# Retention in three fp32r passes: where the kernel now splits scores, masked scores and values into high and low parts

## The reference

```
scores = einsum('bhid,bhjd->bhij', qc, kc) * intra
out    = einsum('bhij,bhjv->bhiv', scores, vc) + einsum('bhid,bhdv->bhiv', qc * q_decay, state)
ret    = head_layer_norm(retention(rq, rk, rv)) * silu(rg)
```

## Time and profile before

| | before |
|---|---|
| median of 3 runs | 2162.86 us (2162.66 to 2163.64) |
| the profiled execution | 2162.67 us |
| its span in the profile | 2160.9 us |
| TensorE matmuls busy | 2127.8 us, 98% |
| VectorE busy | 1155.5 us, 53% |
| ScalarE busy | 775.7 us, 36% |
| granted TensorE clock, mean | 0.998 |

### The profile page before, as it was taken

The page is one execution under the profiler, slowest core; times in us unless marked ns, Lnnn a source line. Parts: engine busy times, 40 slices in busy tenths (PEclk is TensorE's granted clock), DMA queues, the critical chain, the costliest instruction groups (busy, mean ns, idle before and its releaser), DMA issues.

```text
span 2160.9 us, 33274 instructions
## 1 busy us (share of the span) xinstructions
PE 2127.8 (98%) x13064; PEld 1840.4 (85%) x13064; DVE 1155.5 (53%) x1731; ACT 775.7 (36%) x1218; POOL 51.3 (2%) x79
## 2 busy tenths in 40 slices
PE   9999999999999999999999999999999989999998
PEld 8988888788888788888888888989999988889896
DVE  6553334534556455544535666357855557446364
ACT  4222222422444444322324566344433343222233
POOL 0000000000000000000000000012300000000000
PEclk9999999999999999999999999999999999999999
DMA  4222221222222322222223221231133212232222
GB/s 148 97 98 96 93 74 68 89 97 79 75 71 68 107 93 94 98 94 99 88 97 97 79 90 59 83 115 60 55 144 98 88 68 82 95 97 89 96 89 96
DMA packets 52969, 194.71 MB, mean 90 GB/s; under 512 B 6896, under 2 KB 7280, under 8 KB 52224
## 3 DMA queue, kind: packets, MB, share of 16 engines
q1 hardware_dynamic: 49248, 177.56, 24.7%
q10 hardware_dynamic: 2656, 12.41, 1.5%
q0 software_dynamic: 960, 3.24, 0.5%
HBM read 186.77 MB, written 6.42 MB: 89 GB/s over the span
## 4 chain that ended last, share of the span: by engine, by line
PE 94%; DVE 3%; ACT 2%; issue 0%; DMA 0%; SPq 0%; DVEq 0%; ACTq 0%
PE ps L1811 77%; PE ps L2341 5%; PE ps L2208 1%; PE ps L1998 1%; PE ps L2023 1%; PE ps L1961 1%; PE ps L2273 1%; PE ps L2114 1%; DVE kk_r L1456 1%; PE ps L2037 1%; ACT kk L726 1%; ACT kk L727 0%; PE ps L2251 0%; PE ps L2095 0%; PE ps L1940 0%
## 5 line engine op out<-in xcount | busy, mean ns | idle before, releaser
L429 ACT ACTIVATE wh<-wraw 128x1024 fp32r<-128x1024 f32 x330 | 348.4, 1056 | 903.1 <-PE ps L1811 794.8
L986 DVE TENSOR_TENSOR wl<-wraw,wh 128x1024 fp32r<-128x1024 f32 x330 | 403.2, 1223 | 140.9 <-ACT wh L429 133.5
L1811 PE MATMUL ps<-xh,wh 128*128 128x264 f32 (+1 forms) x2056 | 392.4, 336 | 5.9 <-ACT wh L429 2.0
L1811 PE MATMUL ps<-xh,wl 128*128 128x264 f32 (+1 forms) x2056 | 385.6, 332 | 0.0
L1811 PE MATMUL ps<-xl,wh 128*128 128x264 f32 (+1 forms) x2056 | 385.4, 332 | 0.0
L1811 PEld LDWEIGHTS ps<-xh,wh 128*128 128x128 f32 x2056 | 312.5, 188 | 49.4 <-issue 4.8
L1811 PEld LDWEIGHTS ps<-xh,wl 128*128 128x128 f32 x2056 | 314.4, 188 | 39.6
L1811 PEld LDWEIGHTS ps<-xl,wh 128*128 128x128 f32 x2056 | 314.3, 188 | 39.7
L1811 PE MATMUL ps<-bh,wh 128*128 128x264 f32 (+1 forms) x1296 | 234.2, 325 | 2.8 <-DVE hf L1019 1.7
L1811 PE MATMUL ps<-bl,wh 128*128 128x264 f32 (+1 forms) x1296 | 231.0, 322 | 0.0
L1811 PE MATMUL ps<-bh,wl 128*128 128x264 f32 (+1 forms) x1296 | 230.6, 322 | 0.0
(11 more groups left out here) (424 smaller groups left out, 2010.4 us busy)
## 6 DMA issues: line engine op xcount, KB each, us to landing
wraw<-weights_dram SPq DMA_DIRECT2D x331, 512.0 KB, 3.5
hf<-tables_dram POOLq DMA_DIRECT2D x12, 264.0 KB, 3.1
res<-x_t_dram SPq DMA_DIRECT2D x4, 528.0 KB, 7.1
res<-x_t_dram ACTq DMA_DIRECT2D x1, 2112.0 KB, 9.0
res_dram<-res ACTq DMA_DIRECT2D x1, 2112.0 KB, 6.5
mrg_dram<-mrg ACTq DMA_DIRECT2D x1, 2112.0 KB, 7.3
mrg<-mrg_dram ACTq DMA_DIRECT2D x1, 2112.0 KB, 8.8
res<-res_dram ACTq DMA_DIRECT2D x1, 2112.0 KB, 16.0
```

The lines of the kernel that those rows point to most:

```text
L429: nc.scalar.activation(wh[:, slot], wraw[:, slot], ACT.Copy).then_inc(hi_done, 1)
L986: nc.vector.tensor_tensor(wl[:, slot], wraw[:, slot], wh[:, slot].bitcast(F32), ALU.subtract)\
L1811: last = nc.tensor.matmul(o, w[:, slot, c, :], a[:, c, tok], start=(k == 0), stop=(k == len(steps) - 1))
```

## The change

Scores and products of retention are done in three fp32r passes. ScalarE makes the high parts of q and k (turns with step 2 and 3 of the head before, for q and k apart), of the five pieces of the masked scores and of the centred values (both in step 1); VectorE makes the low parts, in the place of the values themselves. The high parts of q, k and the scores lie in `bh`, those of the values in `bl`, which are free until the gated rows are written there. TensorE issues three matmuls where one plain fp32 matmul stood. `products(h, v)` now waits for the low parts of the scores (`ra_lo`) and for the high parts of its values (`rv_hi`), and before its third pass for their low parts (`rv_lo`).

```diff
+        def attention_part(t):
+            q0 = first_query(t)
+            if t == 4:
+                return atm[0:NM, 0:NM], atm_hi[:, :], atm_lo[:, :]
+            return at[:, t, q0:SEQ], at_hi[:, t, q0:SEQ], at_lo[:, t, q0:SEQ]
+        def value_parts(h, v):
+            f, g = slice(RDV * h + P * v, RDV * h + P * v + P), slice(P * v, P * v + P)
+            x, r, y = vt[:, :, f], vtr[:, :, f], values_hi[h % 2][:, :, g]
+            return (x[:, 0:4], y[:, 0:4], r[:, 0:4]), (x[0:NM, 4], y[0:NM, 4], r[0:NM, 4])
...
 ScalarE, turn i, after split_hi
+                h, step = divmod(i - 2, 4)
+                if step < 2 and 0 <= h < RH:
+                    n = RSTRIP + 4 * h + step
+                    act.wait_ge(evicted[n % 2], n // 2 + 1)
+                    if step == 0:
+                        nc.scalar.activation(q_hi[:, NM:T], qq[:, h, NM:T], ACT.Copy).then_inc(rqk_hi, 1)
+                    else:
+                        nc.scalar.activation(k_hi, qq[:, 4 + h, :], ACT.Copy).then_inc(rqk_hi, 1)
                 h, step = divmod(i - 4, 4)
                 if step == 1 and 0 <= h < RH:
+                    for t in range(5):
+                        whole, high, _ = attention_part(t)
+                        act.wait_ge(rs_masked, 5 * h + t + 1)
+                        nc.scalar.activation(high, whole, ACT.Copy).then_inc(ra_hi, 1)
                     for v in range(2):
...
+                    act.wait_ge(centred, h + 1)
+                    for v in range(2):
+                        for whole, high, _ in value_parts(h, v):
+                            ins = nc.scalar.activation(high, whole, ACT.Copy)
+                        ins.then_inc(rv_hi, 1)
...
 VectorE, step 1
+                    attention_low(h)
                     centred_values(h)
+                    values_low(h, 0)
+                    values_low(h, 1)
...
             def products(h, v):
-                pe.wait_ge(centred, h + 1)
+                pe.wait_ge(ra_lo, 5 * h + 5)
+                pe.wait_ge(rv_hi, 2 * h + v + 1)
...
+                for k in range(3):
+                    if k == 2:
+                        pe.wait_ge(rv_lo, 2 * h + v + 1)
+                    V, A = (1, 1, 2)[k], (1, 2, 1)[k]
+                    for t in range(4):
+                        q0 = first_query(t)
+                        nc.tensor.matmul(ps[:, 5 + v, q0:SEQ], main[V][:, t], attention_part(t)[A], start=(t == k == 0),
+                                         stop=False)
```

More of the change, by code:

```diff
@@ L137, in build @@
         wh, wl = sb("wh", [P, 2, KC, P], F32R), sb("wl", [P, 2, KC, P], F32R)
-        qq = sb("qq", [P, KC, T])
+        qq, qqr = shared("qq", [P, KC, T])
         kk, kkr = shared("kk", [P, KC, T])
-        vt = sb("vt", [P, 5, D])
+        vt, vtr = shared("vt", [P, 5, D])
         mrg = sb("mrg", [P, KC, T])
-        res = sb("res", [P, KC, T])
+        res, resr = shared("res", [P, KC, T])
         tmp = sb("tmp", [P, 2, T])
@@ L237, in build @@
         rz_ready, rs_masked, ro_ready, ro_copied = (sem(n) for n in ("rz_ready", "rs_masked", "ro_ready", "ro_copied"))
+        rqk_hi, rqk_lo, ra_hi, ra_lo, rv_hi, rv_lo = (sem(n) for n in ("rqk_hi", "rqk_lo", "ra_hi", "ra_lo", "rv_hi",
+                                                                      "rv_lo"))
         centred, rsq_added, rsum_done, r_scaled = (sem(n) for n in ("centred", "rsq_added", "rsum_done", "r_scaled"))
@@ L306, in scores_ap @@
             return (ps[:, 2, :], ps[:, 3, 0:400], ps[:, 4, 0:272], ps[:, 4, 272:416], ps[0:NM, 4, 416:432])[t]
+        at_lo, atm_lo = flat(resr)[:, 0:4 * SEQ].rearrange("p (k q) -> p k q", k=4), flat(resr)[0:NM, 4 * SEQ:4 * SEQ + NM]
+        at_hi, atm_hi = flat(bh)[:, 0:4 * SEQ].rearrange("p (k q) -> p k q", k=4), flat(bh)[0:NM, 4 * SEQ:4 * SEQ + NM]
+        q_hi, k_hi = flat(bh)[:, 4 * T:5 * T], flat(bh)[:, 5 * T:6 * T]
+        values_hi = [flat(bl)[:, 5 * RDV * k:5 * RDV * (k + 1)].rearrange("p (t f) -> p t f", t=5) for k in range(2)]
+        def attention_part(t):
[7 more added lines that the diff above has]
+            return (x[:, 0:4], y[:, 0:4], r[:, 0:4]), (x[0:NM, 4], y[0:NM, 4], r[0:NM, 4])
         ret_silu = {21: (0, 1, 2), 22: (3, 4, 5), 23: (6,), 24: (7,)}
@@ L1200, in centred_values, with attention_low, values_low @@
                     .then_inc(centred, 1)
+            def attention_low(h):
+                for t in range(5):
+                    whole, high, low = attention_part(t)
+                    dve.wait_ge(ra_hi, 5 * h + t + 1)
+                    nc.vector.tensor_tensor(low, whole, high.bitcast(F32), ALU.subtract).then_inc(ra_lo, 1)
+            def values_low(h, v):
+                dve.wait_ge(rv_hi, 2 * h + v + 1)
+                for whole, high, low in value_parts(h, v):
+                    ins = nc.vector.tensor_tensor(low, whole, high.bitcast(F32), ALU.subtract)
+                ins.then_inc(rv_lo, 1)
             for i in range(N_RET + 3):
@@ L1207, in _ @@
                     split_lo(n, n // 2, n % 2)
+                h, step = divmod(i - 2, 4)
+                if step < 2 and 0 <= h < RH:
+                    dve.wait_ge(rqk_hi, 2 * h + step + 1)
+                    if step == 0:
+                        nc.vector.tensor_tensor(qqr[:, h, NM:T], qq[:, h, NM:T], q_hi[:, NM:T].bitcast(F32), ALU.subtract)\
+                            .then_inc(rqk_lo, 1)
+                    else:
+                        nc.vector.tensor_tensor(qqr[:, 4 + h, :], qq[:, 4 + h, :], k_hi.bitcast(F32), ALU.subtract)\
+                            .then_inc(rqk_lo, 1)
                 h, step = divmod(i - 4, 4)
@@ L1931, in scores @@
             def scores(h):
-                for j in (4 * h, 4 * h + 1, 4 * h + 2):
-                    n = RSTRIP + j
-                    pe.wait_ge(evicted[n % 2], n // 2 + 1)
+                n = RSTRIP + 4 * h + 2
+                pe.wait_ge(evicted[n % 2], n // 2 + 1)
+                pe.wait_ge(rqk_lo, 2 * h + 2)
                 if h:
                     pe.wait_ge(vt_done, 2 * h)
+                q_lo, k_lo = qqr[:, h, :], qqr[:, 4 + h, :]
                 for t in range(5):
                     q0 = first_query(t)
-                    keys = qq[:, 4 + h, P * t:P * t + P] if t < 4 else qq[:, 4 + h, SEQ:T]
-                    ins = nc.tensor.matmul(scores_ap(t), keys, qq[:, h, NM + q0:T] if t < 4 else qq[:, h, SEQ:T],
-                                           start=True, stop=True)
+                    for j, (k_, q_) in enumerate(((k_hi, q_hi), (k_hi, q_lo), (k_lo, q_hi))):
+                        ins = nc.tensor.matmul(scores_ap(t), k_[:, P * t:min(P * t + P, T)], q_[:, NM + q0:T],
+                                               start=(j == 0), stop=(j == 2))
                     if t in (0, 1, 4):
@@ L1954, in products @@
             def products(h, v):
-                pe.wait_ge(centred, h + 1)
+                pe.wait_ge(ra_lo, 5 * h + 5)
+                pe.wait_ge(rv_hi, 2 * h + v + 1)
                 if h:
                     pe.wait_ge(ro_copied, 2 * (h - 1) + v + 1)
[L1958 to L1963, removed]
+                main, last_rows_ = value_parts(h, v)
+                for k in range(3):
[6 more added lines that the diff above has]
+                                         stop=False)
+                    ins = nc.tensor.matmul(ps[:, 5 + v, SEQ - NM:SEQ], last_rows_[V], attention_part(4)[A], start=False,
+                                           stop=(k == 2))
+                ins.then_inc(ro_ready, 1)
             def ret_sums(h):
```

## The result

| | before | after |
|---|---|---|
| median, 17 runs each | 2162.97 us (2162.48 to 2163.65) | 2166.77 us (2166.01 to 2168.56) |
| span of the profiled execution | 2160.9 us | 2164.6 us |
| granted TensorE clock, mean | 0.998 | 0.998 |

The ratio is 1.0017, with a 95% interval of 1.0011 to 1.0023. The change costs 3.8 us where I had forecast a gain of 1.8, and the time lies 0.6 us above the range. The difference is under 0.2%, as most of the chances said, but it is resolved, and of the other sign. One execution of the kernel before, among the 21 beside three of the experiments, took 2991.61 us at a mean granted clock of 0.653, and the ratios leave it out.

The account below looks back on a forecast made before the run. TensorE was taken as the bound, with 94% of the chain. Its work shrinks 5.6 us, waits add 3.7 and the strip behind 0.15: -1.75 us, a median of 2161.1 us, range 2157.3 to 2166.2.

Parts of the forecast that it names:

- the price of a pass: Retention products on TensorE: one fp32r pass 0.75 us, three 2.26, saving 0.50 us on each of eight products.
- Scores: Retention's four scores on TensorE: 2.56 us each before, a saving of 0.4 us each (0.30 to 0.45).
- Waits: TensorE ahead of each head's first product, held by ScalarE and VectorE hand-overs: 1.5, 0.64, 0.64, 0.9 us, 3.7 in all.
- T + 8.4: Start of a head's first product, in us after its transposes start (T); before, T + 7.76 in heads 2 and 3.
- The strip behind the first product: It waits for VectorE's late eviction, starting at T + 10.7, product ending T + 10.66: 0.05 us in three heads, 0.15 in all.
- The strip's extra 0.1: Extra time of the strip behind scores and products, counted in their old prices and expected to vanish.
- the clock: Rival 2: TensorE's four waits in retention throttle its clock, up to +6.6 us, 2167.7; chance 5%.
- narrow matmuls: Rival 1, retention: matmuls at the rate of their columns, pass 0.61 us, 3.3 us more gained, 2157.8; chance 6%.
- the chain: Retention's hand-overs through three engines: each head waits 1.5 us more than in the sum, 2168 or so; chance 10%.
- both bounds: Whole kernel: 2157.3 us if all waits were hidden, 2165.8 if no instruction on the path overlapped the next.
- rival 3: Longer chain through three engines, 10%, about 2168; at 0.3 us an ACTIVATE, five copies 2.6 us, 2165.1 in all.
- Signs of being wrong: Retention: first-product wait over 2.5 us, eviction later than product, second wait for q and k parts, pass not 0.75 us.

Follow-up runs that it names:

- e2: The changed kernel with the last block of each retention product over 128 rows, zeros below the 16: 2160.91 us.
- e1: The changed kernel with the three 16-row matmuls of each retention product moved together to its end: 2162.78 us.
- e9: The changed kernel with the last block of each retention product over 64 rows, zeros below the 16: 2167.14 us.
- e5: The kernel before the change, with the last block of each retention product over 128 rows, zeros below the 16: 2160.60 us.
- e6: The kernel before the change, with three fp32r passes in the scores alone, splits of q and k included, products left in plain fp32: 2160.92 us.
- e3: The changed kernel with the high and low parts of the masked scores made a turn earlier, right behind the masks: 2162.84 us.

## Why the prediction was wrong

The step that failed is the price of a pass: "The other four stand side by side in the stick-breaking stage: from 1250.42 to 1250.94, 0.52 us. A pass is thus 0.75 us, three 2.26 us. This saves 0.50 us a product." The row of 16 columns there has weights of 128 rows; in a product the last block has 16 columns and 16 rows. I matched the moving side and not the weights. The pass took 1.0 us, so a product 3.02 us in place of 2.26: 8 x 0.76 = 6.1 us, against a gap of 5.7 between forecast (2161.1) and result (2166.77). Of the 0.76 us, e2 gives back 0.71 with 128 rows; e1, e2 and e9 show the cause.

The kernel before has the same joint, where the old product ends with its 16 rows:

```profile
276.21 0.39 PE L1962 MATMUL ps<-res,vt 16*128 16x16 f32 x2
276.53 2.20 PE L1811 MATMUL ps<-xh,wh 128*128 128x264 f32 x16
```

From the 16 rows to the strip it is 0.32 us. Over 128 rows the same step is 0.14 (284.62 to 284.76 in e5). I had taken these 0.32 us into the price of the old product and not into that of the new passes.

Point by point, the others held but for small amounts:

- *Scores*: saving of 0.4 forecast (0.30 to 0.45), 0.47 measured, just above the bound; their last block has 16 columns of weights, but all 128 rows. e6 confirms it alone: 2.3 us with four of them.
- *Waits*: 1.5, 0.64, 0.64 and 0.9 us forecast, 3.7 in all. Measured from where the strip lets go: 274.95 - (271.55 + 1.93) = 1.47 in head 1, 308.57 - (306.09 + 1.93) = 0.55 in head 2, the same in head 3, 0.79 in head 4: 3.4. T + 8.4 was T + 8.3. e3 shows that there are none without the parts of the scores ahead of the values.
- *The strip behind the first product*: eviction forecast from T + 9.85, measured T + 9.87. No wait showed.
- *The strip's extra 0.1*, taken as a cost of plain fp32 and so as a gain: it stayed. This is part of the 0.76.
- *Rivals*: the clock stayed (granted 0.998), narrow matmuls did not go at the rate of their columns, the chain was not longer. None of the rivals had the mechanism that decided; it is a fifth one, on TensorE's own work, where I had set both bounds from passes of even rows. The 0.3 us an ACTIVATE that rival 3 takes from the Trainium skill (ScalarE: Activation LUTs, Rules for kernel authors) is given there for a bias that is a pointer operand, and these copies pass none; the five took 1.58 us (301.49 to 303.07, where the first copy of the values starts), as the sum had it (1.6) and not 2.6.
- *Signs of being wrong*: of those that the prediction named one came, a pass that is not 0.75 us.

With the measured prices the sum is right: products 8 x (3.02 - 2.76) = +2.1 and 0.3 for the late load behind four waits, scores -1.9, waits +3.4: +3.9 us; the spans differ by 3.7, the medians by 3.8.

## What to carry to other kernels

When a matmul is priced from a row of another stage, its weights must match too, rows as well as columns, and not only the width that moves. A short block of keys between full ones (16 or 64 rows between 128) cost about 0.24 us in fp32r and 0.31 in plain fp32 for each change of rows and back; pad it with zeros to 128 rows, or put such blocks side by side, and look for them before splitting a product in passes, which multiplies them. New work in a queue goes where that engine idles, not where its result is used: ten instructions of 0.2 to 0.6 us in front of a hand-over, in each of four heads, cost 3.9 us, and one turn earlier no wait.

## What I had not expected of the hardware

Between matmuls of 128 rows, a matmul of 16 x 16 is dearer than one of 128 rows and 16 columns: over 64 rows it costs the same as over 16 (2167.14 and 2166.77 us), over 128 rows the kernel takes 2160.91. Three of them side by side cost a product about as much over even rows as one joint does (e1: 2.56 us a product, with one joint, against 2.31 without and 3.02 with three).
